# Gate and up products of a two-layer transformer's feed-forward blocks, computed with the weights standing in the array

## The reference, cut to what matters

```python
D_MODEL, SEQ, DEPTH, D_FF = 1024, 256, 2, 2816

def _swiglu(x, w_gate, w_up, w_down):
    return (jax.nn.silu(x @ w_gate) * (x @ w_up)) @ w_down

for l in range(DEPTH):
    x = x + 0.5 * _swiglu(_rmsnorm(x, ffn1_norm[l]), ffn1_w_gate[l], ffn1_w_up[l], ffn1_w_down[l])
    ...                       # the mixer: three attention branches, gates, output product
    x = x + 0.5 * _swiglu(_rmsnorm(x, ffn2_norm[l]), ffn2_w_gate[l], ffn2_w_up[l], ffn2_w_down[l])
return _rmsnorm(x, final_norm)
```

## Time and profile before

| | us |
|---|---|
| median of three runs | 1186.78 |
| the profiled execution | 1186.27 |
| its span in the trace | 1184.5 |
| PE busy / PE weight loads busy | 1176.3 / 962.6 |
| DVE busy / ACT busy | 732.6 / 582.6 |

### The profile page before, as it was taken

How to read it: one execution, slowest core, us unless ns; L and a number is a source line. 1 busy time by engine, 2 the same in 40 slices (tenths; PEclk the granted TensorE clock), 3 DMA queues, 4 the chain that set the end, 5 groups by cost and what they waited for, 6 DMA issues and landing times.

```text
span 1184.5 us, 16306 instructions
## 1 busy us (share of the span) xinstructions
PE 1176.3 (99%) x5761; PEld 962.6 (81%) x5761; DVE 732.6 (62%) x1038; ACT 582.6 (49%) x759; POOL 32.2 (3%) x67
## 2 busy tenths in 40 slices
PE   9999999999999999999999999999999999999997
PEld 6888888888777888888888888888877788888886
DVE  5545546769977565445564454477798685644554
ACT  6444345447764454443454444454578645434433
POOL 2000000001000000000000000000010000000000
PEclk9999999999999999999999999999999999999999
DMA  8655564755424565565546555646553344655560
GB/s 286 213 188 201 177 194 143 244 191 164 138 73 177 178 206 185 178 199 190 176 160 205 199 181 177 199 157 190 196 178 108 140 147 159 230 177 184 193 207 36
DMA packets 148991, 210.98 MB, mean 178 GB/s; under 512 B 8160, under 2 KB 109136, under 8 KB 148944
## 3 DMA queue, kind: packets, MB, share of 16 engines
q1 hardware_dynamic: 148256, 209.64, 53.9%
q10 hardware_dynamic: 688, 0.71, 0.2%
HBM read 209.28 MB, written 1.05 MB: 178 GB/s over the span
## 4 chain that ended last, share of the span: by engine, by line
PE 99%; DMA 0%; DVE 0%; issue 0%; ACT 0%; POOLq 0%; POOL 0%; SPq 0%; DVEq 0%
PE ps L1275 29%; PE ps L1277 29%; PE ps L1276 29%; PE ps L1485 2%; PE ps L1388 2%; PE ps L1513 1%; PE ps L1541 1%; PE ps L1325 1%; PE ps L1294 1%; PE ps L1446 1%; DMA raw<-in_ffn_w_gate_dram 0%; PE ps L1458 0%; PE ps L1572 0%; PE ps L1532 0%; DVE x L916 0%
## 5 line engine op out<-in xcount | busy, mean ns | idle before, releaser
L492 DVE TENSOR_TENSOR wlo<-raw,whi 128x2048 fp32r<-128x2048 f32 (+1 forms) x195 | 436.8, 2245 | 221.4 <-ACT whi L1030 196.9
L1275 PE MATMUL ps<-whi,ht_hi 128*128 128x512 f32 (+1 forms) x1192 | 470.7, 395 | 0.0
L1277 PE MATMUL ps<-whi,ht_lo 128*128 128x512 f32 (+1 forms) x1192 | 461.6, 387 | 0.0
L1276 PE MATMUL ps<-wlo,ht_hi 128*128 128x512 f32 (+1 forms) x1192 | 460.6, 386 | 0.0
L1030 ACT ACTIVATE whi<-raw 128x2048 fp32r<-128x2048 f32 (+1 forms) x195 | 365.2, 1877 | 181.3 <-PE ps L1277 181.2
L1277 PEld LDWEIGHTS ps<-whi,ht_lo 128*128 128x128 f32 x1192 | 223.9, 188 | 46.7
L1275 PEld LDWEIGHTS ps<-whi,ht_hi 128*128 128x128 f32 x1192 | 224.1, 188 | 43.0 <-issue 0.8
L1276 PEld LDWEIGHTS ps<-wlo,ht_hi 128*128 128x128 f32 x1192 | 224.4, 188 | 42.4
L1275 PE MATMUL ps<-whi,at_hi 128*128 128x512 f32 x336 | 131.4, 391 | 0.0
L1277 PE MATMUL ps<-whi,at_lo 128*128 128x512 f32 x336 | 130.9, 390 | 0.0
L1276 PE MATMUL ps<-wlo,at_hi 128*128 128x512 f32 x336 | 130.8, 389 | 0.0
(11 more groups left out here) (169 smaller groups left out, 703.9 us busy)
## 6 DMA issues: line engine op xcount, KB each, us to landing
raw<-in_ffn_w_down_dram SPq DMA_DIRECT2D x88, 512.0 KB, 3.9
raw<-in_w_in_dram SPq DMA_DIRECT2D x88, 512.0 KB, 4.5
raw<-in_ffn_w_gate_dram SPq DMA_DIRECT2D x85, 512.0 KB, 4.0
raw<-in_ffn_w_up_dram SPq DMA_DIRECT2D x85, 512.0 KB, 4.9
raw<-in_w_out_dram SPq DMA_DIRECT2D x16, 512.0 KB, 4.4
raw<-in_w_branch_c_dram SPq DMA_DIRECT2D x8, 512.0 KB, 4.2
raw<-in_w_branch_b_dram SPq DMA_DIRECT2D x4, 512.0 KB, 4.0
raw<-in_w_branch_a_dram SPq DMA_DIRECT2D x4, 512.0 KB, 4.1
```

Source lines behind the costliest of these rows:

```text
L492: nc.vector.tensor_tensor(wlo[:, n, 0:w], raw[:, n, 0:w], whi[:, n, 0:w].bitcast(F32), ALU.subtract).then_inc(lo_done, 1)
L1275: nc.tensor.matmul(o, xh, wh, start=start, stop=False)
L1276: nc.tensor.matmul(o, xh, wl, start=False, stop=False)
L1277: return nc.tensor.matmul(o, xl, wh, start=False, stop=stop)
```

## The change

The roles in `gate_up` are exchanged. 128 columns of the weight stand in the array, and the 256 rows of x pass by. x's high part and rest lie side by side (`ht`, 512 columns for each block k), so that one matmul of 512 columns makes high weight by both parts of x, the two results in the two halves of a bank; a second one of 256 columns makes the weight's rest by the high part of x, into the first half. For each of the 8 blocks k there are four weight blocks j (two of gate, two of up), each with its own bank, so that a step has 32 matmuls of 512 columns (L1403) and 32 of 256 (L1406). The result has inner values on the partitions, and `turn` and its semaphore go.

What the product still needs is done by other instructions. The two halves of each bank are added: for gate by a DVE sum over pairs (`gates_out`, reads 1024 elements per partition and writes 512), for up by an ACT copy of the first half (`up_part`) and a DVE addition of the second (`ups_out`). `rstd` now belongs to a column, so that it must be turned and spread over all partitions once for each FFN: two matmuls in the second slab of step 1 (`turn_scales`, which waits until step 0's banks are read) and a DVE copy into `scale_t`. DVE multiplies the gates by it (`scaled_gates`); ACT's Silu, DVE's product, the rounding and the rest then work on 128x512 in SBUF. For up the factor is moved into `residual`, whose factor is now `hrstd` (half of `rstd`). A step uses banks 0 to 3; step 0 uses 4, 5, 0, 1 and step 1 uses 6, 7, 2, 3, so that the first down (into 4 to 7) waits in its middle until DVE has read the gates of step 1. Step 1 stands outside of ACT's and DVE's loops.

```diff
-        ht_hi = sb("ht_hi", [P, KD, SEQ], F32R)
-        ht_lo = sb("ht_lo", [P, KD, SEQ], F32R)
+        ht = sb("ht", [P, KD, 2, SEQ], F32R)
+        ht_hi, ht_lo = ht[:, :, 0, :], ht[:, :, 1, :]
...
+        def step_banks(i):
+            return {0: (4, 5, 0, 1), 1: (6, 7, 2, 3)}.get(i, (0, 1, 2, 3)) if isinstance(i, int) else (0, 1, 2, 3)
...
+            def gates_out(l, f, i):
+                wait_used(dve, l, (f * (FFN_SLABS + MIX_SLABS) + 3 * i if i else f * (FFN_SLABS + MIX_SLABS) + 1)
+                          if isinstance(i, int) else (i, f * (FFN_SLABS + MIX_SLABS)))
+                g = step_banks(i)[0]
+                nc.vector.tensor_reduce(sg, ps[:, g:g + 2, :].rearrange("p j (h c) -> p j c h", h=2), AX_X,
+                                        ALU.add).then_inc(gu_out, 1)
+
+            def scaled_gates(l, f, i):
+                dve.wait_ge(gu_out, (l * 2 + f) * (2 * NSTEP) + i * 2 + 1)
+                nc.vector.tensor_tensor(sg, sg, scale_t.unsqueeze(1).broadcast_to([P, 2, SEQ]), ALU.mult)                    .then_inc(gu_scaled, 1)
+
+            def ups_out(l, f, i):
+                dve.wait_ge(up_out, (l * 2 + f) * NSTEP + i + 1)
+                u = step_banks(i)[2]
+                nc.vector.tensor_tensor(act, act, ps[:, u:u + 2, SEQ:2 * SEQ], ALU.add).then_inc(gu_out, 1)
+
             def products(l, f, i):
-
                 r = l * 2 + f
-                for t in range(NT):
-                    dve.wait_ge(silu_done, r * (2 * NSTEP) + i * 2 + t + 1)
...
-                    nc.vector.scalar_tensor_tensor(act[:, t, :], ps[:, bank, FSTEP:2 * FSTEP], rstd[:, t:t + 1],
-                                                   sg[:, t, :], ALU.mult, ALU.mult).then_inc(act_done, 1)
+                dve.wait_ge(silu_done, r * NSTEP + i + 1)
+                dve.wait_ge(gu_out, r * (2 * NSTEP) + i * 2 + 2)
+                nc.vector.tensor_tensor(act, act, sg, ALU.mult).then_inc(act_done, 1)
...
+                convert(l, s0 + 3)
+                gates_out(l, f, 0)
+                ups_out(l, f, 0)
+                dve.wait_ge(scale_ps, l * 2 + f + 1)
+                nc.vector.tensor_copy(scale_t, ps[:, 0, 0:SEQ]).then_inc(scale_sb, 1)
+                dve.wait_ge(scale_sb, l * 2 + f + 1)
+                scaled_gates(l, f, 0)
                 products(l, f, 0)
-                convert(l, s0 + 3)
                 act_rest(l, f, 0)
...
+                    for j in range(4):
+                        nc.tensor.matmul(ps[:, banks[j], :], wv[:, kk, j * P:(j + 1) * P],
+                                         ht[:, k, :, :].rearrange("p a c -> p (a c)"), start=k == 0, stop=False,
+                                         skip_group_check=True)
+                        ins = nc.tensor.matmul(ps[:, banks[j], 0:SEQ], wr[:, kk, j * P:(j + 1) * P], ht_hi[:, k, :],
+                                               start=False, stop=k == KD - 1, skip_group_check=True)
...
+            def turn_scales(l, f):
+
+                pe.wait_ge(rstd_ready, (l * 3 + 2 * f) * 3 + 3)
+
+                pe.wait_ge(gu_out, (l * 2 + f) * (2 * NSTEP) + 2)
+                for t in range(NT):
+                    ins = nc.tensor.matmul(ps[:, 0, t * P:(t + 1) * P], rstd[:, t:t + 1].broadcast_to([P, P]),
+                                           ident[:, :], start=t == 0, stop=t == 1, skip_group_check=True)
+                ins.then_inc(scale_ps, 1)
...
-                wide(l, s0 + 2, 0, 4, (0, 1), 512, 0, KD - 1, pieces=l == f == 0)
-                turn(l, f, 0)
-                wide(l, s0 + 3, 4, 4, (0, 1), 512, 0, KD - 1)
-                down(l, f, 0, s0 + 4, start=True)
-                turn(l, f, 1)
+                turned_wide(l, s0 + 2, 0, step_banks(1), False, between={3: lambda: turn_scales(l, f)}, pieces=l == f == 0)
+                turned_wide(l, s0 + 3, 4, step_banks(1), False)
+
+                down(l, f, 0, s0 + 4, True, {2: lambda: pe.wait_ge(gu_out, (l * 2 + f) * (2 * NSTEP) + 3)})
                 with pe.Fori(2, last) as i:
                     gate_up(l, f, i)
                     down(l, f, i - 1, (i, s0 + 1))
-                    turn(l, f, i)
                 gate_up(l, f, last)
-                down(l, f, last - 1, s0 + 3 * last + 1, between={2: lambda: turn(l, f, last)})
+                down(l, f, last - 1, s0 + 3 * last + 1)
```

More of the change, by code:

```diff
@@ L585, in one @@
                         convert(l, (r, s0 + c + 3))
-                    if not isinstance(i, int):
+                    if not final(i):
+                        products(l, f, i)
                         act_rest(l, f, i)
-                with dve.Fori(1, NSTEP - 1) as i:
+                one(1)
+                with dve.Fori(2, NSTEP - 1) as i:
                     one(i)
@@ L1100, in one @@
                     convert(l, (r, s0 + c + 2))
-                    silu(l, f, i, False)
+                    up_part(l, f, i)
+                    silu(l, f, i)
+                    if final(i):
+                        act_round(l, f, i)
                     if not end:
                         convert(l, (r, s0 + c + 3))
-                    act_round(l, f, i)
-                with eng.Fori(1, NSTEP - 1) as i:
+                    if not final(i):
+                        act_round(l, f, i)
+                one(1)
+                with eng.Fori(2, NSTEP - 1) as i:
                     one(i)
@@ L1298, in prep, with turned_wide, weights @@
                     ins.then_inc(xt_ps, 1)
-            def by_pieces(l, s, kk, k, first, banks, wh, wl, start, stop):
-                def weights(sem, whole):
+            def turned_wide(l, s, k0, banks, first, n=0, between={}, pieces=False):
+                if not pieces:
+                    ready(l, s)
+                wv = whi[:, slot(s), :].rearrange("p (k c) -> p k c", k=4)
+                wr = wlo[:, slot(s), :].rearrange("p (k c) -> p k c", k=4)
+                def weights(kk, sem, whole):
                     if (s, kk) in PIECE:
@@ L1333, in wide @@
+                ins.then_inc(slab_used, 1)
+            def wide(l, s, k0, nk, banks, width, kstart, kstop, first=False, n=0, between={}):
+                ready(l, s)
                 wv = whi[:, slot(s), 0:nk * width].rearrange("p (k c) -> p k c", k=nk)
@@ L1338, in wide @@
                         between[kk]()
-                    if pieces:
-                        ins = by_pieces(l, s, kk, k, first, banks, wv[:, kk, :], wr[:, kk, :], k == kstart, k == kstop)
-                        continue
                     if first:
```

167 lines of the change are left out of this document (89 added, 78 removed).

## The result

The changed kernel takes 1197.16 us (median of four runs, 1196.93 to 1197.33), the kernel before 1186.62 beside it (1186.35 to 1186.83). The ratio is 1.0089 [1.0071, 1.0106]: slower by 10.5 us, where I had said 1184.5 and a range up to 1193. The figures of the changed kernel come from its profiled execution, 1197.33 us with a span of 1195.6.

A forecast was written before the change was run, and what follows sets the result against it. PE's own instruction distances were taken as the bound. Steps -11.7, starts +5.2, second FFNs' scales +0.5, first FFN +1.7, scale matmuls 4 x 0.22, ends +1.35 made -2.1 us from 1186.27: 1184.2, stated as 1184.5, range 1173 to 1193.

The forecast's parts named there:

- PE alone bounds the kernel, and PE waits nowhere in steps 2 to 9: Whole kernel: time is the sum of PE's instruction distances; ACT and DVE keep 1 us margin in steady steps.
- The turn, 0.48 us a step: Each FFN step: removing the transposes, with the slower distances behind them, saves 0.48 us, 21.1 us over 44 steps.
- No distance shorter than 111.5 ns: Earlier trace: no pair of weight load and matmul was read as closer than 111.5 ns, agreeing with the 107 ns load.
- What comes: t = 0.1201, a pair 0.3468: Gate and up: a 256-column matmul takes 0.1201 us, 0.3468 with a wide one; a step gains 0.27 us, 44 steps 11.7.
- Down's matmuls at 0.2267: Down product of each step: 24 matmuls of 512 columns stay 0.2267 us apart, 5.44 us together.
- The second rival: Gate and up: narrow matmuls can't hide the next load, t = 0.1257; steps gain 3.8 us, total 1192.1; chance 0.20.
- The starts, 1.3 us in each FFN: First down of each FFN: PE waits 0.7 us for DVE's slab and 0.6 for step 1's gates; 5.2 in four.
- The scale matmuls, 0.22 us in each FFN: Step 1 of each FFN: PE's matmuls that turn the scales add 0.22 us, four times.
- The second FFNs' wait for the scales, 0.25 us, twice: Second FFN of each layer: PE asks for the scales before DVE's addition ends, waiting 0.25 us; 0.5 in all.
- The first FFN, 1.7 us: Program's first FFN: PE waits 1.5 us at the scales, 1.7 with the shift before, after taking off earlier waits.
- The ends, 0.45 us in three FFNs: Behind the last step: DVE's mixer slab delays x's additions and splitting, 0.45 us in three FFNs (1.35), 0 in the last.
- The sum: Whole kernel: all terms make -2.1 us against the profiled 1186.27, giving 1184.2, stated as 1184.5; chance 0.45.

The follow-up runs named there:

- noturn: The kernel before without the four transposes of each step, the untransposed product being rounded and split from SBUF: 1165.81 us, ratio 0.9825.
- g16: The changed kernel with gate and up matmuls grouped for each slab, 16 of 512 columns then 16 of 256, instead of alternating: 1187.38 us.
- best: g16 plus, at each FFN's start, the first down's slab converted ahead of the scale chain, and behind FFNs the mixer's second slab after x's first rest: 1186.33 us.

## Why the prediction was wrong, by its own steps

- **PE alone bounds the kernel, and PE waits nowhere in steps 2 to 9.** Right. DVE rose from 62% to 70% without a wait in the loop, and the sum over pairs took 1.224 us on the page (mean of 44), where 1.22 was taken.
- **The turn, 0.48 us a step.** Right: 0.47 by `noturn`.
- **No distance shorter than 111.5 ns.** This reading of the earlier trace rows holds for the mean of the row alone: the first distance of that row, behind a wide matmul, is 0.10 us, and the transposes of the earlier trace rows start 0.11 apart. Nothing in the sum rests on it.
- **What comes: t = 0.1201, a pair 0.3468.** This step failed, not in t but in the sum of a pair, and in taking one price for every step. I priced narrow ones as among themselves and wide ones as among themselves. That held for some stretches of steps 0 and 1 (0.3467). In steps 2 to 10 a pair took 0.3528, just outside of the 0.352 that I had named as proof against me: 32 x 6.0 ns x 36 = 6.9 us. `g16`, with the same matmuls in rows of like ones, has the forecast price there. Why alternation has two prices, and why these steps fall into the higher one, stays open. The evidence was on my table: in the earlier trace rows matmuls of 512 columns behind four short ones take 0.230 for 13 intervals. I read from it that the overhead depends on how load and matmul meet, charged it to the turn, and didn't ask what a short one between every two would do.
- **Down's matmuls at 0.2267.** Off behind the same pairs: the first ones are slower behind narrow ones, 5.50 for 5.44 us, 2.2 us over 36 steps. With the pairs it is (16.79 - 16.54) x 36 = 9.0 us of the 13.1 between the forecast for the profiled execution (1184.2) and its 1197.33. `g16` takes 0.22 of these 0.25 us a step back.
- **The second rival had the sign and came nearer in time (1192.1, 5 us off), with a wrong mechanism.** 0.1194 to 0.120 for the narrow ones among themselves, and a surplus that stays at 384 and 448 columns, speak against it.
- **The starts, 1.3 us in each FFN.** Right. In layer 1's first FFN the two waits stand in PE's timeline of the changed kernel:

```profile
623.91 0.28 PE L1406 MATMUL ps<-ht,wlo 128*128 128x256 f32 x1
624.71 0.47 PE L1331 MATMUL ps<-whi,at_hi 128*128 128x512 f32 x1 [0.51 <-DVE wlo L503]
625.01 0.39 PE L1332 MATMUL ps<-wlo,at_hi 128*128 128x512 f32 x1
```

  Less the undisturbed distances (0.117 + 0.227) the first costs 1.10 - 0.34 = 0.76. The second, for the gates of step 1 in the middle of down, stands at 627.95; it costs 0.97 - 0.45 = 0.52 in the same way. 0.7 and 0.6 were forecast. DVE's chain there runs in the forecast order.

- **The scale matmuls, 0.22 us in each FFN.** Too low. In PE's timeline of the changed kernel the two matmuls of plain float32 stand as four instructions, here in layer 0's second FFN and in layer 1's first:

```profile
427.44 0.28 PE L1406 MATMUL ps<-ht,wlo 128*128 128x256 f32 x1
427.86 0.68 PE L1464 MATMUL ps<-ident,rstd 128*128 128x128 f32 x4
428.61 0.28 PE L1406 MATMUL ps<-ht,wlo 128*128 128x256 f32 x1
...
616.40 0.28 PE L1406 MATMUL ps<-ht,wlo 128*128 128x256 f32 x1
616.52 0.61 PE L1464 MATMUL ps<-ident,rstd 128*128 128x128 f32 x4
617.20 0.28 PE L1406 MATMUL ps<-ht,wlo 128*128 128x256 f32 x1
```

  At 616, where PE doesn't wait, it is 0.80 us from narrow to narrow, of which a narrow and a wide one are 0.35: the scale matmuls cost 0.45 where 0.22 was taken, some 0.9 us more over four FFNs. The 1.17 at 427 holds a wait besides.
- **The second FFNs' wait for the scales, 0.25 us, twice.** Right. The list of waits has only the first FFN's at L1464, but the distances show two more: from the last narrow matmul to the first scale matmul it is 427.86 - 427.44 = 0.42 us (0.42 also at 1017.46 in layer 1's second FFN), and 616.52 - 616.40 = 0.12 where nothing waits. DVE's addition of step 0 runs until 427.7, just ahead of the first scale matmul. That is 0.3 us each.
- **The first FFN, 1.7 us.** Low: its wait for the scales is 1.8 alone. Up to step 2 the stage lost 4.6 us where 2.7 were forecast (1.3 + 1.7 + 0.22, less the gain of two steps). Which part of the first slabs has the rest I haven't taken apart.
- **The ends, 0.45 us in three FFNs.** 0.6 each, and 0.3 in the last, where 0 was forecast. DVE's queue there, in the changed kernel:

```profile
192.50 2.29 DVE L503 TENSOR_TENSOR wlo<-raw,whi 128x2048 fp32r<-128x2048 f32 x1 [1.17 <-ACT whi L1072]
194.71 1.41 DVE L547 SCALAR_TENSOR_TENSOR x<-ps,hrstd,x 128x512 f32<-128x512 f32 x2
```

  x's first columns are added only behind a whole slab, as forecast; the sum of the small delays was put too low.
- **The sum.** By the parts of the FFNs: 1184.2 + 8.9 (steps 2 to 10) + 3.4 (starts) + 0.8 (ends) = 1197.3, as measured. Of the starts' 3.4 the scale matmuls are 0.9, and 1.7 lie in the first FFN beyond them; what makes up the rest isn't shown.

## What to carry to other kernels

Price a matmul by its distance in the company it will have: take the distance of unlike neighbours from a place where the trace has them, and where it has none, give it a range that reaches above the sum of the two kinds. When matmuls of two lengths can be ordered freely, try the equal ones in long rows (at 512 and 256 columns rows of 16 brought 9.8 us and rows of 4 brought 3.9; at 512 and 128 they brought nothing), then look at what each row now asks for earlier than before. Before adding up two gains, look whether the first run's trace still has the wait that the second is to remove. A kernel that is all PE is decided by nanoseconds a matmul: 6 ns a pair, and what the pairs do to the down matmuls behind them, are 9 of the 13 us between forecast and result, and the starts nearly all of the rest.

## What the runs showed of the hardware that I had not expected

- fp32r matmuls of 512 columns with a load each are 0.2267 us apart among themselves, and 0.224 to 0.236 for the first five behind 16 of 256 columns and the first ten behind 16 of 128. Alternated with 256 columns a pair takes 0.3467 or 0.353, steady over a stretch, for the same instructions. Why stays open; load floor, change of bank and layout each fell by a run of their own.
- Among themselves 256 columns take 0.120 us, and 220 and 128 both 0.112, so that below some width fewer columns save nothing.
- Two matmuls of plain float32 with 128 columns are four instructions.
- PE's clock can drop where PE waits long. `g16`'s profiled execution has it in the first FFN (two stretches of 4 us: busy time of PE, weight loads, DVE, ACT and POOL, granted clock, DMA share, GB/s):

```profile
22.00:26.00 4.00, 1.54 (x7) 0.94 (x5) 3.96 (x3) 0.22 (x1) 0.00 (x0) 1.00 0.90 279
26.00:30.00 4.00, 3.89 (x16) 3.54 (x17) 1.81 (x3) 0.77 (x2) 0.00 (x0) 0.57 0.73 250
```

  PE was busy for 1.54 of 4 us, with a wait of 2.6 in them, and in the next 4 us the granted clock was 0.57, for most of them at the lower of its two levels (1.2 of 2.4 GHz). From the first scale matmul to the first wide one of the next slab, the same 24 matmuls take 31.02 - 26.11 = 4.91 us there and 29.73 - 26.39 = 3.34 in the profiled execution of `best`, so that 1.6 were lost on top of the wait. `best` has the same wait (2.55) and kept the full clock in it, so the wait alone doesn't decide. Of `g16`'s ten runs, the four with a granted clock of 0.999 took 1186.1 to 1186.2 us and the six with 0.997 or 0.998 took 1187.4 to 1187.9.
